# Attention in steps of two query blocks, in a two-layer encoder kernel on one NeuronCore

## What is computed

```python
def dense_attention(q, k, v, scale):              # groups A and B
    sc = einsum('bhqd,bhkd->bhqk', q, k) * scale  # blocks of 128 queries, 512 keys
    return einsum('bhqk,bhkd->bhqd', softmax(sc), v)

# A: 4 heads of width 64, each o1 - lam * o2 of two dense attentions with keys of width 32
# B: 6 heads, keys of width 64 + 32 (the 32 rotated, shared by the heads), values of width 64
# C: 6 heads of width 64, three dilated bands whose results are weighted by their softmax sums
out_a = diff_attention(a_q, a_k, a_v, ...)
out_b = mla_attention(b_cq, b_ckv, b_kr, ...)
out_c = dilated_attention(c_q, c_k, c_v, pos)
mix = concatenate([out_a, out_b, out_c], axis=-1) @ w_o[l]
```

## Time and profile before

| | us |
|---|---|
| median of 3 runs | 3279.19 |
| lowest and highest | 3278.62, 3279.29 |
| the profiled execution, its own time | 3279.06 |
| its span, first to last instruction | 3277.2 |
| PE busy | 3176.5 (97%) |
| DVE busy | 2534.8 (77%) |
| POOL busy | 1956.5 (60%) |
| ACT busy | 1307.2 (40%) |
| mean granted clock of PE | 0.991 |

### The profile page before, as it was taken

How to read it: one execution, slowest core, us unless ns; L and a number is a source line. 1 busy time by engine, 2 the same in 40 slices (tenths; PEclk the granted TensorE clock), 3 DMA queues, 4 the chain that set the end, 5 groups by cost and what they waited for, 6 DMA issues and landing times. The chain is left out here.

```text
span 3277.2 us, 64226 instructions
## 1 busy us (share of the span) xinstructions
PE 3176.5 (97%) x18582; PEld 2888.5 (88%) x18582; DVE 2534.8 (77%) x5431; ACT 1307.2 (40%) x2080; POOL 1956.5 (60%) x1556
## 2 busy tenths in 40 slices
PE   8998999999999999999999999999999999999997
PEld 8877889999999888888798787899999998888886
DVE  1475557888888899999925756588888888999998
ACT  2364234444434333333324642344444443333332
POOL 3454348888654466666544543488886545666665
PEclk9999999999999999999999999999999999999999
DMA  4002139999787799999820012499997877999996
GB/s 162 36 2 78 48 99 316 317 323 319 243 301 254 252 337 339 335 337 336 279 103 26 2 78 58 124 319 320 322 319 242 290 242 274 339 337 337 337 333 226
DMA packets 249405, 765.22 MB, mean 233 GB/s; under 512 B 28384, under 2 KB 95712, under 8 KB 241376
## 3 DMA queue, kind: packets, MB, share of 16 engines
q1 hardware_dynamic: 170400, 459.95, 42.3%
q0 software_dynamic: 73728, 268.47, 22.0%
q10 hardware_dynamic: 5184, 35.65, 3.0%
HBM read 677.98 MB, written 85.98 MB: 233 GB/s over the span
## 5 line engine op out<-in xcount | busy, mean ns | idle before, releaser
L696 POOL TENSOR_TENSOR st_lo<-st_raw,st_hi 128x1024 fp32r<-128x1024 f32 x290 | 697.6, 2406 | 463.6 <-ACT st_hi L966 460.0
L966 ACT CAST st_hi<-st_raw 128x1024 fp32r<-128x1024 f32 x544 | 569.7, 1047 | 659.0 <-PE ps L2063 659.0
L1972 PE MATMUL ps<-t_hi,st_hi 128*128 128x384 f32 (+1 forms) x2288 | 794.6, 347 | 0.0
L1973 PE MATMUL ps<-t_lo,st_hi 128*128 128x384 f32 (+1 forms) x2288 | 786.6, 344 | 0.0
L804 POOL TENSOR_TENSOR wt_lo<-w_f,wt_hi 128x384 fp32r<-128x384 f32 x256 | 417.4, 1630 | 318.1 <-ACT wt_hi L1097 318.0
L1976 PE MATMUL ps<-t_hi,st_lo 128*128 128x384 f32 (+1 forms) x2288 | 462.3, 344 | 0.0
L1973 PEld LDWEIGHTS ps<-t_lo,st_hi 128*128 128x128 f32 x2288 | 430.2, 188 | 10.2
L1972 PEld LDWEIGHTS ps<-t_hi,st_hi 128*128 128x128 f32 x2288 | 430.1, 188 | 9.9
L1976 PEld LDWEIGHTS ps<-t_hi,st_lo 128*128 128x128 f32 x2288 | 408.2, 188 | 10.7
L1009 ACT ACTIVATE h_out<-ps 128x384 f32<-128x384 f32 x256 | 125.8, 491 | 693.9 <-PE ps L1976 616.6
L2063 PE MATMUL ps<-st_hi,wt_hi 128*128 128x512 f32 x1536 | 390.0, 389 | 2.7 <-ACT wt_hi L1097 2.7
(11 more groups left out here) (222 smaller groups left out, 4972.9 us busy)
## 6 DMA issues: line engine op xcount, KB each, us to landing
st_raw<-in_peer_u SPq DMA_DIRECT2D x256, 512.0 KB, 4.4
st_raw<-in_peer_v SPq DMA_DIRECT2D x256, 512.0 KB, 4.6
gelu_d<-h_out SPq DMA_DIRECT2D x256, 192.0 KB
h_in<-gelu_d SPq DMA_DIRECT2D x256, 192.0 KB, 5.4
gates_d<-g_stage ACTq DMA_DIRECT2D x32, 1024.0 KB, 5.8
g_ch<-gates_d SPq DMA_DIRECT2D x56, 512.0 KB, 6.1
w_raw<-in_w_in SPq DMA_DIRECT2D x16, 1168.0 KB, 5.3
st_raw<-in_peer_w_q SPq DMA_DIRECT2D x32, 512.0 KB, 3.7
```

The costliest lines, as they stand in the source:

```text
L696: nc.gpsimd.tensor_tensor(st_lo[:, s].rearrange("p c f -> p (c f)"), st_raw[:, r], st_hi[:, s].rearrange("p c f -> p (c f)").bitcast(F32), ...
L966: nc.scalar.copy(st_hi[:, r % 2].rearrange("p c f -> p (c f)"), st_raw[:, r]).then_inc(st_h, 1)
L1972: nc.tensor.matmul(dst, st_hi[:, s, c], t_hi[:, c, rows], start=c == 0, stop=False)
L1973: nc.tensor.matmul(dst, st_hi[:, s, c], t_lo[:, c, rows], start=False, stop=False)
```

## The change

PE takes two blocks at a time: two scores, then two blocks of transposes (`two_blocks`); then the heads of the job after next, or a value step of two blocks. Half a job before stood between two value steps; now a pair of jobs has two value steps instead of four. The heads of job j + 2 are turned in the middle of job j instead of at its end, and ACT's `scale_q` and DVE's `keep_k` for them move with them. The values of pair i - 1 are multiplied in the second half of each job of pair i. The turn back of pair i - 2 stands in the middle of the even job of pair i, after the heads; before, that of pair i - 1 stood in the odd job of pair i. ACT's `keep_ot` and DVE's `finish` move likewise. The number of instructions that compute is the same; POOL's and SP's queues are unchanged.

```diff
--- before.py
+++ after.py
@@ -927,25 +927,25 @@
             def job(j):
 
                 s = j % 2
-                more = j + 1 < JOBS
-                if more:
-                    scale_q(j + 1, 1 - s, KINDS[(j + 1) // 2])
                 exponent(j, s, 3)
+                keep_pt(j, s, 1)
+                if j + 2 < JOBS:
+                    scale_q(j + 2, s, KINDS[j // 2 + 1])
+                if j + 1 < JOBS:
+                    exponent(j + 1, 1 - s, 0)
                 if j == JOBS - 1:
                     keep_ot(PAIRS - 2)
-                keep_pt(j, s, 1)
-                if s == 1 and 1 < j < JOBS - 1:
-                    keep_ot(j // 2 - 1)
-                if more:
-                    exponent(j + 1, 1 - s, 0)
+                elif s == 0 and j >= 4:
+                    keep_ot(j // 2 - 2)
+                if j + 1 < JOBS:
                     exponent(j + 1, 1 - s, 1)
+                    exponent(j + 1, 1 - s, 2)
                 keep_pt(j, s, 3)
-                if more:
-                    exponent(j + 1, 1 - s, 2)
 
             scale_q(0, 0, "A")
             for qb in range(AHEAD):
                 exponent(0, 0, qb)
+            scale_q(1, 1, "A")
             for j in range(JOBS):
                 job(j)
             keep_ot(PAIRS - 1)
@@ -1262,28 +1262,30 @@
 
             def job(j):
 
-                s, kind = j % 2, KINDS[j // 2]
+                s = j % 2
                 ahead = KINDS[(j + 1) // 2] if j + 1 < JOBS else None
-                if ahead is not None:
-                    keep_k(j + 1, 1 - s, ahead)
-                score(j, 3, kind)
-                keep_pt(j, s, 0)
+                score(j, 3, KINDS[j // 2])
                 if j > 0:
                     invert_sums(j - 1, 1 - s, (j - 1) // 2 % 2)
                 if ahead is not None:
                     score(j + 1, 0, ahead)
+                keep_pt(j, s, 0)
+                if j + 2 < JOBS:
+                    keep_k(j + 2, s, KINDS[j // 2 + 1])
+                if ahead is not None:
                     score(j + 1, 1, ahead)
                 if j == JOBS - 1:
-                    finish(PAIRS - 2, (PAIRS - 2) % 2)
-                keep_pt(j, s, 2)
-                if s == 1 and 1 < j < JOBS - 1:
-                    finish(j // 2 - 1, (j // 2 - 1) % 2)
+                    finish(PAIRS - 2, PAIRS % 2)
+                elif s == 0 and j >= 4:
+                    finish(j // 2 - 2, j // 2 % 2)
                 if ahead is not None:
                     score(j + 1, 2, ahead)
+                keep_pt(j, s, 2)
 
             keep_k(0, 0, "A")
             for qb in range(AHEAD):
                 score(0, qb, "A")
+            keep_k(1, 1, "A")
             for j in range(JOBS):
                 job(j)
 
@@ -1834,16 +1836,17 @@
                 c0 = COL_C + 2 * C_W + (2 * (i - PAIRS_A - PAIRS_B) + s) * CDK
                 return h[:, k, c0:c0 + CDK]
 
-            def values(i, qb):
-
-                if qb == 0:
+            def values(i, half):
+
+                if half == 0:
                     pe.wait_ge(o_ev, PAIRS * l + i)
-                pe.wait_ge((pt_dve, pt_act)[qb % 2], 2 * (JOBS * l + 2 * i + 1) + qb // 2 + 1 + 1)
-                for k in range(TB):
-                    for s in range(2):
-                        last = nc.tensor.matmul(ps[s * VD:(s + 1) * VD, O_BANK, qb * P:(qb + 1) * P], value_of(i, s, k),
-                                                p_t[:, (2 * i + s) % PT, qb, k], start=k == 0, stop=k == TB - 1)
-                if qb == TB - 1:
+                for qb in (2 * half, 2 * half + 1):
+                    pe.wait_ge((pt_dve, pt_act)[qb % 2], 2 * (JOBS * l + 2 * i + 1) + half + 1 + 1)
+                    for k in range(TB):
+                        for s in range(2):
+                            last = nc.tensor.matmul(ps[s * VD:(s + 1) * VD, O_BANK, qb * P:(qb + 1) * P], value_of(i, s, k),
+                                                    p_t[:, (2 * i + s) % PT, qb, k], start=k == 0, stop=k == TB - 1)
+                if half == 1:
                     last.then_inc(pv_done, 1)
 
             def turn_back(i):
@@ -1858,86 +1861,56 @@
                 if j < JOBS:
                     turn_qk(j, j % 2, KINDS[j // 2])
 
-            def even(i):
-
-                j, kind = 2 * i, KINDS[i]
-                score(j, 0, 3, kind)
-                turn_p(j, 0)
-                if i > 0:
+            def two_blocks(j, half):
+
+                s = j % 2
+                more = j + 1 < JOBS
+                if half == 0:
+                    score(j, s, 3, KINDS[j // 2])
+                    if more:
+                        score(j + 1, 1 - s, 0, KINDS[(j + 1) // 2])
+                elif more:
+                    score(j + 1, 1 - s, 1, KINDS[(j + 1) // 2])
+                    score(j + 1, 1 - s, 2, KINDS[(j + 1) // 2])
+                turn_p(j, 2 * half)
+                turn_p(j, 2 * half + 1)
+
+            def pair(i):
+
+                two_blocks(2 * i, 0)
+                turn_ahead(2 * i + 2)
+                if i >= 2:
+                    turn_back(i - 2)
+                two_blocks(2 * i, 1)
+                if i >= 1:
                     values(i - 1, 0)
-                score(j + 1, 1, 0, kind)
-                turn_p(j, 1)
-                if i > 0:
+                two_blocks(2 * i + 1, 0)
+                turn_ahead(2 * i + 3)
+                two_blocks(2 * i + 1, 1)
+                if i >= 1:
                     values(i - 1, 1)
-                score(j + 1, 1, 1, kind)
-                turn_p(j, 2)
-                if i > 0:
-                    values(i - 1, 2)
-                score(j + 1, 1, 2, kind)
-                turn_p(j, 3)
-                turn_ahead(j + 2)
-
-            def odd(i):
-
-                j, kind = 2 * i + 1, KINDS[i]
-                ahead = KINDS[i + 1] if i + 1 < PAIRS else None
-                score(j, 1, 3, kind)
-                turn_p(j, 0)
-                if i > 0:
-                    values(i - 1, 3)
-                if ahead is not None:
-                    score(j + 1, 0, 0, ahead)
-                turn_p(j, 1)
-                if ahead is not None:
-                    score(j + 1, 0, 1, ahead)
-                turn_p(j, 2)
-                if i > 0:
-                    turn_back(i - 1)
-                if ahead is not None:
-                    score(j + 1, 0, 2, ahead)
-                turn_p(j, 3)
-                turn_ahead(j + 2)
-
-            def last_even(i):
-
-                j, kind = 2 * i, KINDS[i]
-                score(j, 0, 3, kind)
-                turn_p(j, 0)
+
+            def last_pair(i):
+
+                two_blocks(2 * i, 0)
+                turn_back(i - 2)
+                two_blocks(2 * i, 1)
                 values(i - 1, 0)
-                score(j + 1, 1, 0, kind)
-                turn_p(j, 1)
                 values(i - 1, 1)
-                score(j + 1, 1, 1, kind)
-                turn_p(j, 2)
-                values(i - 1, 2)
-                score(j + 1, 1, 2, kind)
-                turn_p(j, 3)
-                values(i - 1, 3)
-
-            def last_odd(i):
-
-                j = 2 * i + 1
-                score(j, 1, 3, KINDS[i])
-                turn_p(j, 0)
+                two_blocks(2 * i + 1, 0)
                 turn_back(i - 1)
-                turn_p(j, 1)
-                turn_p(j, 2)
+                two_blocks(2 * i + 1, 1)
                 values(i, 0)
-                turn_p(j, 3)
                 values(i, 1)
+                turn_back(i)
 
             turn_qk(0, 0, "A")
             for qb in range(AHEAD):
                 score(0, 0, qb, "A")
             turn_ahead(1)
             for i in range(PAIRS - 1):
-                even(i)
-                odd(i)
-            last_even(PAIRS - 1)
-            last_odd(PAIRS - 1)
-            for qb in range(2, TB):
-                values(PAIRS - 1, qb)
-            turn_back(PAIRS - 1)
+                pair(i)
+            last_pair(PAIRS - 1)
 
             pe.wait_ge(mix_ready, l + 1)
             for tb in range(TB):
```

## The result

| | us |
|---|---|
| before, median of 4 runs beside it | 3278.90 (3277.91 to 3279.29) |
| after, median of 4 runs | 3305.73 (3305.33 to 3306.38) |
| ratio after to before, 95% interval | 1.0085 [1.0073, 1.0097] |
| profiled execution after: its time, its span | 3306.38, 3304.6 |

The change makes the kernel 27 us slower, 0.85%. The forecast was 3306, with a range of 3289 to 3318.

A forecast was written before the change was run, and what follows sets the result against it. PE bounds the attention. Per layer, gains of -12.6 us and added waits of +18.6 net +6.0, +12 for both; with +15 for the clock, 3279.06 becomes 3306 us, range 3289 to 3318.

The forecast's parts named there:

- The wait at B: PE's turn back of `o_t` starts 3.0 us after the heads' start, held by ACT: 8 x 2.12 = +17.0 us per layer.
- `finish` at V: PE's value step waits for DVE's `finish`, 0.35 us in two pairs, 0.1 in three: +1.0 us per layer.
- Today's waits: PE's existing waits go, 0.49 us at three turn backs, 1.1 in two later pairs: together -4.1 per layer.
- The gain of fewer value steps: On PE, each value step fewer saves 0.355 us of change-over: -7.0 us per layer.
- The first pairs: Pair 1, with no turn back yet, goes from 13.2 to 11.3 us; a wait in the first pair adds 0.4.
- The clock: PE's clock falls to half speed behind 10 of the 16 new waits, at 1.5 us each: +15 us.
- Rival 3: ACT hands `o_t` over before PE wants it, so only the gains stand: 3255 us, chance 0.06.
- Its turning point: At the turn back, a wait of 12 / 8 = 1.5 us; below that the change wins.
- Rival 1: The same waits at the turn back, but the clock never falls: 3291 us, chance 0.09.
- rival 2: Every new wait at the turn back makes the clock fall: 3318 us, chance 0.07.

The follow-up runs named there:

- experiment 1: Changed kernel with ACT copying `o_t` ahead of `scale_q`: 3277.3 us, ratio 0.9994 to the kernel before.
- experiment 2: Changed kernel with ACT copying `o_t` between `scale_q` and the exponent: 3284.69 us, ratio 1.0018 to the kernel before.
- experiment 4: Also called kernel 4: changed kernel with turn back ahead of heads, `o_t` copy first in ACT's job, `finish` ahead of `keep_k`: 3256.14 us, ratio 0.993 to before.
- experiment 5: Kernel 4 with the value steps of pairs 1 to 8 split into steps of one block: 3266.08 us, 9.9 us more than kernel 4.
- experiment 3: Changed kernel with sixteen unused identity transposes on PE ahead of each turn back in pairs 2 to 9: 3296.58 us, ratio 1.0051 to the kernel before.

## Why the prediction was right, and which of its steps were not

**The wait at B: right, in mechanism and size.** 3.0 us from H's start worked out, 3.06 found. The prediction priced B's delay over H's eight transposes, 2.12 us; like for like that is 3.06 - 0.88 = 2.18 in kind A and 2.98 - 0.88 = 2.10 in kind B. The waits as the rows count them, from H's end, are 1.95 to 2.19 us, 32 us in all. Experiments 1, 2 and 4 take instructions out of the chain, and the time follows: 3296.6 with the whole chain and no fall, 3284.7 without the exponent, 3277.3 without `scale_q` too, 3256.1 without a wait.

**`finish` at V: right.** 0.43 us in pair 3 against 0.35, 0.19 in kind C against 0.1. Kinds B and C came out at 17.65 and 16.02 for 17.6 and 15.9, kind A at 14.53 for 14.3.

**Today's waits: right in sum, not in every place.** "0.49 at B in three A pairs": the turn back of the third, pair 3, waited 0.03 us (193.59 in the kernel before), and 0.44 us stood ahead of the first score of kind B behind it (191.05) instead. Pairs 7 and 8 had the 1.1 us of waits each that were worked out, pair 6 had 0.52 where 0.4 was taken.

**The gain of fewer value steps: right in kind, 0.05 too large.** 0.30 for each (experiment 5) instead of 0.355. For 16 of them that is 0.9 us per layer.

**The first pairs: under-counted.** The step that failed here is "pair 1, which has no B yet, 13.2 to 11.3". It added up PE's rows alone; the earlier trace rows had DVE and ACT at 15.3 and 13.1 of 20 us in a pair that still had its values and took 16.4 us, and this does not hold for one without. Measured 12.76: 1.46 too little per layer, and 0.2 to 0.35 more in pair 0.

**The clock: over-counted.** The prediction took 10 of 16 at 1.5 us each; the runs show 7 of 16 at 1.3 us, 9.2 us for 15. The earlier trace rows had one fall at 1.33 us and one hold at 1.81 us. In the kernel after the seven falls follow waits of 1.95 to 2.19 us, and the nine that passed are as long, so the length alone does not decide. Each fall begins 0.2 to 1.5 us behind the start of its B. Experiment 2 had sixteen of 1.25 to 1.49 us without a fall; but at the attentions' starts, where several waits follow one another, layer 2 of the kernel before had one behind 1.10 and 0.87 us (at 1772), and kernel 4 had none behind waits up to 2.20 us. Which of the waits lose the clock I can't derive.

**The sum.** The attentions without the falls grew by 26.2 - 9.2 = 17.0 us where 12 was forecast: 3.5 from the first pairs, 1.8 from the value steps, -0.3 from the rest. The clock is 5.8 under its term. What lies outside the attentions, 1.1 us, no experiment touched. So 12 + 15 = 27.0 against 17.0 + 9.2 + 1.1 = 27.3: the total agrees better than its parts, since an error of 5 us and one of 5.8 cancelled. That 3306 was hit within 1 us is luck; that the kernel would be slower, and by the waits at B, is not.

**The rivals.** Rival 3's price, 3255, is what kernel 4 takes within 1.2 us, in part by luck: the first pairs gained less than forecast, and the falls at the starts that its profiled execution lacks made up for it. Its turning point was wrong: it put it at a wait of 1.5 us, while waits of 0.77 us in the mean (experiment 1) gave 3277.3 and of 1.31 us (experiment 2) 3284.7; between them 3279 lies at about 0.9 us. It was not the gain that was too large: kernel 4 has 23 us of it, 1.44 us for each of 16 turn backs. But 12 / 8 sets all of it against B's wait. A wait at B costs some 0.25 us more than its row shows (experiment 4), and experiments 1 and 2 have 4.1 and 2.9 us of waits for `finish` beside it, 0.18 to 0.26 for each turn back. Rival 1, no falls, was forecast at 3291 and measured at 3296.6 by experiment 3, for the reasons under the sum; rival 2, every wait a fall, is excluded by the nine that were none.

## What to carry to other kernels

Before a step is moved on the engine that bounds, follow what feeds it through the other engine's queue: the instructions ahead of its copy there count, and above all the first of them that can't start before the step's new neighbour has ended. The order that wins 23 us with the turn back ahead of the heads loses 27 with it behind them. And where work is missing, as in the first pairs, ask again which engine bounds, since the busy shares of a full stretch don't hold there.

## What the runs showed of the hardware

- A wait of PE can cost more than its length: seven falls to 1.2 GHz cost 1.1 to 1.6 us each, behind waits of 2 us in an attention where PE was otherwise busy. Of equal waits some are followed by a fall and others not, and none of the sixteen of 1.25 to 1.49 us in experiment 2 was.
- Transposes of an identity matrix, with no use but to keep PE from standing still, held the clock at 2.4 GHz and won 9.15 us (experiment 3).
- Leaving the transposes for a value step (128 by 64) and coming back costs 0.30 us beyond the matmuls' own time. In the Trainium skill, "TensorEngine Tiling (Array Packing)", Key Properties, has it that a change of tiling mode makes the engine drain. The runs show a cost at the change and its size; that a drain makes it, they do not show.
